# A two-block transformer kernel: expert rows added into X by TensorE inside the expert loop, and the cross attention's value projection moved behind the experts

## The chip, the cores and the metric

One core of one Trainium2 chip runs the whole program. The metric is device time in microseconds, the median of the runs shown. A core has TensorE (matrix products, PE in the rows), VectorE (DVE), ScalarE (ACT), GpSimd (POOL) and SyncE (SP), which only issues transfers. All of them run their own instruction stream and meet at semaphores.

## The reference

Two blocks follow one another on x of 512 tokens by 1024. Only the parts around the change are shown; everything is fp32.

```python
# first block: attention, then the experts
h2 = rms_norm(x, norm2_g[l]) * (1.0 + scale2) + shift2
# each token takes 2 of 32 experts (1024 -> 512 -> 1024); weights = g_prob * softmax(top 2 logits)
def expert_block(xb, e):
    return (jax.nn.silu(xb @ w_gate[e]) * (xb @ w_up[e])) @ w_down[e]
out = jnp.zeros((t, d)).at[row_token].add(ys * row_weight[:, None])
x = x + gate2[:, None, :] * out
x = rms_norm(x, final_norm_g)
# second block
h = rms_norm_2(x, norm_mix_g);  x = x + hybrid_mixer(h, ...)      # convolution and sparse attention
h = rms_norm_2(x, norm_x_g);    x = x + cross_attention(h, mem, xq_w, xkv_w, xo_w)
h = rms_norm_2(x, norm_ffn_g);  x = x + swiglu(h, ffn_in_w, ffn_out_w)
return rms_norm_2(x, final_norm_g_2)
# in cross_attention: mem is 256 x 1024 and does not depend on x
k, v = jnp.split(mem @ wkv, 2, axis=-1)
```

## The kernel before

**Experts.** The 32 experts run as 16 pairs: expert p on array columns 0 to 63 and expert p + 16 on columns 64 to 127, with at most 64 tokens each (CAP). What does not fit would go through an overflow loop, which these inputs do not enter. For pair p, GpSimd gathers 128 rows of h2 from DRAM by `idx[:, p]` (L2559). TensorE runs `moe_up` (gate into bank 0, up into bank 1, L1037), then the transposes of the next pair's rows (`moe_transpose_x`, L1019), the transposes of a (`moe_transpose_a`, L1046) and `moe_down` (banks 4 and 5, L1058). ACT applies SiLU and copies the transposed rows (L1593, L1586); VectorE multiplies (`moe_multiply`, L2215), copies the transposed a (`moe_keep_a`, L2207) and multiplies the result with gate2 into Y (`moe_keep_y`, L2223). ACT's queue stores Y to `expert_rows` in DRAM (`moe_store`, L1597). Weights have one buffer per kind: slots 0 and 1 gate, 2 and 3 up, 4 and 5 down. SP issues the next gate, up and down pieces (L538) as soon as the semaphores `gate_full`, `up_full` and `down_full` tell that the old ones are used. All expert products are fp32.

**Adding the rows to X.** After pair 14 is stored, GpSimd gathers the rows of the pairs 0 to 14 for each token (eight indirect transfers, L2567), and VectorE adds each with its weight into X (`expert_rows`, L2241). Rows of the last pair are not stored; TensorE multiplies them by a weighted selection matrix (`weighted_rows`, L1086, fp32) and VectorE adds the banks (L2248). Since the gather may also name overflow rows, a stretch of zeros was stored into `expert_rows` early in the attention (L521). The weighted selection is formed by VectorE after the routing (`selection`, L2176 to L2181) and transposed by TensorE (L1007, kept at L2199).

**Between the blocks.** ACT squares X with sums (`norm`, L1408), VectorE scales X with the final gain (L2311), ACT squares again, VectorE writes the scaled XN4 (L1862), TensorE transposes it (L775), ACT and VectorE split it into high and low parts (L1444, L1884), and the first projection of the second block (glu_g0) starts.

**Projections of the second block.** Each fp32 product is three fp32r products of split operands (`split_product`, L720 to L722). A weight chunk of 2 MiB (1024 x 512) lies in one of two slots in turn. It is handled in two halves: ACT rounds a half to its high part (`split_weights`, L1436, two buffers), GpSimd subtracts to form the low part (`low_weights`, L2513), and TensorE uses both. A table (`HALVES`) names for every half what must be done before its high buffer is taken again: `half_used` for first halves, `proj_done` of the chunk for second halves. SP loads chunk c when the chunk before it in the same slot is used (`chunk`, L488). The order on ACT, GpSimd, SP and TensorE is written out by hand.

**Cross attention.** Its order was: transposes of mem (L775) with their split (L1761, L2452), key projection (`xk`, L1767), norm of X, value projection (`xv`, two chunks of two token tiles, L1773), transposes of the normed X, query projection (`xq`).

## Time and profile before

| | |
|---|---|
| median of 3 runs | 2162.72 us (2159.34 to 2164.78) |
| profiled execution, its own time | 2158.53 us |
| its span, first to last instruction | 2156.7 us |
| mean granted TensorE clock | 0.946 of 2.4 GHz |
| busy: TensorE, VectorE, ACT, GpSimd | 88%, 31%, 27%, 29% of the span |
| bytes moved by DMA | 379.24 MB, mean 176 GB/s |

The execution can be cut by time: attention of the first block until about 385 us, routing until 432, experts until 922, norms until 955, then the second block; its cross attention begins at 1573. A busy share says little by itself: each stage has its own limit, and what counts there is which wait ends last. The rows further down show start and duration in microseconds, and in square brackets how long the engine sat idle before and who ended that.

### The profile page before, as it was taken

The numbers are of one execution on the slowest core, as the hardware profiler recorded it, in microseconds if no ns is written. First come the engines' busy times: TensorE is split into PE (matmuls) and PEld (weight loads), VectorE is DVE, ScalarE is ACT, GpSimd is POOL, SyncE is SP. The second block draws the span as 40 slices with busy tenths as digits, with TensorE's granted clock in tenths as the row PEclk, the third lists the DMA queues.
The fourth block names the chain that finished last, engine by engine and source line by source line (L and its number), as shares of the span: only waits on it lengthen the run. The fifth ranks groups of instructions, "written<-read, shape, count | busy, mean of one in ns | idle before, by whom it ended". The sixth has DMA issues, their size and how long they took to land.

```text
span 2156.7 us, 21339 instructions
## 1 busy us (share of the span) xinstructions
PE 1900.6 (88%) x8492; PEld 1229.5 (57%) x8492; DVE 671.8 (31%) x1383; ACT 582.9 (27%) x1042; POOL 629.6 (29%) x361
## 2 busy tenths in 40 slices
PE   4999989488778778769999999888889889999997
PEld 2544337333222222248888878544677578888886
DVE  6551265610011001155897024465211211000001
ACT  3113462110000000042231243566243423222211
POOL 0001233300000000124442224555364324555532
PEclk8999899699999999989997998999999999999999
DMA  9453301889999999932222312000233122232221
GB/s 376 156 229 110 124 1 64 331 338 424 428 428 427 430 428 428 424 131 93 103 86 71 120 57 98 20 21 21 98 122 113 40 88 78 78 112 84 94 102 59
DMA packets 94291, 379.24 MB, mean 176 GB/s; under 512 B 6219, under 2 KB 35275, under 8 KB 79868
## 3 DMA queue, kind: packets, MB, share of 16 engines
q1 hardware_dynamic: 88176, 356.99, 42.5%
q0 software_dynamic: 3456, 12.58, 1.5%
q10 hardware_dynamic: 2572, 8.46, 1.0%
q8 instruction: 60, 0.98, 0.2%
q14 instruction: 27, 0.22, 0.0%
HBM read 357.50 MB, written 20.51 MB: 175 GB/s over the span
## 4 chain that ended last, share of the span: by engine, by line
PE 70%; DMA 16%; DVE 7%; ACT 4%; issue 2%; POOL 1%; SPq 0%; DVEq 0%; ACTq 0%; POOLq 0%
PE bank L720 14%; PE bank L722 14%; PE bank L721 14%; DMA slots<-in_w_expert_up 14%; PE bank L695 11%; PE bank L1037 6%; PE bank L1252 2%; PE bank L1232 1%; PE bank L848 1%; ACT area L1749 1%; POOL low_r L2513 1%; DMA slots<-in_w_ada 1%; PE bank L766 1%; PE bank L1221 1%; PE bank L775 1%
## 5 line engine op out<-in xcount | busy, mean ns | idle before, releaser
L2513 POOL TENSOR_TENSOR low_r<-slots,high_r 128x2048 fp32r<-128x2048 f32 x87 | 401.1, 4611 | 605.7 <-ACT high_r L1436 605.7
L721 PE MATMUL bank<-xl_r,high_r 128*128 128x512 f32 (+1 forms) x864 | 330.6, 383 | 0.0
L720 PE MATMUL bank<-area_r,high_r 128*128 128x512 f32 x800 | 314.2, 393 | 0.0
L1037 PE MATMUL bank<-slots,area 128*64 128x512 f32 x992 | 247.0, 656 | 75.6 <-DMA slots<-in_w_expert_gate 39.0
L722 PE MATMUL bank<-area_r,low_r 128*128 128x512 f32 x800 | 312.5, 391 | 0.0
L1436 ACT ACTIVATE high_r<-slots 128x2048 fp32r<-128x2048 f32 x87 | 166.2, 1913 | 434.7 <-PE bank L722 413.8
L1037 PEld LDWEIGHTS bank<-slots,area 128*64 128x64 f32 x992 | 76.8, 151 | 245.2 <-issue 151.1
L721 PEld LDWEIGHTS bank<-xl_r,high_r 128*128 128x128 f32 x864 | 163.4, 189 | 31.9 <-issue 0.5
L720 PEld LDWEIGHTS bank<-area_r,high_r 128*128 128x128 f32 x800 | 151.1, 189 | 31.9 <-issue 0.5
L722 PEld LDWEIGHTS bank<-area_r,low_r 128*128 128x128 f32 x800 | 150.9, 189 | 31.6
L2339 DVE SCALAR_TENSOR_TENSOR bank<-area,cols,bank 128x512 f32<-128x512 f32 x232 | 153.4, 747 | 0.0
L695 PE MATMUL bank<-slots,area 128*128 128x512 f32 (+2 forms) x384 | 132.7, 499 | 2.0 <-ACT slots L1523 1.3
L1058 PE MATMUL bank<-slots,area 128*64 128x512 f32 x512 | 115.1, 602 | 19.3 <-DMA slots<-in_w_expert_down 8.7
L2559 POOL DMA_INDIRECT area<-h_rows,idx x16 | 15.6, 973 | 396.8 <-PE bank L1019 381.1
L722 PE MATMUL bank<-high_r,area_r 128*128 128x512 f32 x304 | 120.8, 397 | 0.0
L2215 DVE TENSOR_TENSOR area<-bank,area 128x512 f32<-128x512 f32 x16 | 11.1, 692 | 322.6 <-PE bank L1037 322.6
L695 PEld LDWEIGHTS bank<-slots,area 128*128 128x128 f32 x384 | 67.4, 193 | 60.0 <-issue 56.0
L695 PE MATMUL bank<-area 64*128 64x512 f32 (+3 forms) x150 | 72.1, 676 | 19.5 <-ACT area L1454 13.0
L1593 ACT ACTIVATE area<-bank 128x512 f32<-128x512 f32 x16 | 9.6, 597 | 291.4 <-PE bank L1037 291.4
L1058 PEld LDWEIGHTS bank<-slots,area 128*64 128x64 f32 x512 | 37.6, 138 | 85.7 <-issue 81.9
L2603 POOL TENSOR_SCALAR area<-area,small 128x128 f32<-128x128 f32 (+3 forms) x112 | 64.4, 585 | 69.4 <-DVE small L2418 69.4
L2484 DVE TENSOR_TENSOR area<-bank,area 128x512 f32<-128x512 f32 x22 | 15.2, 692 | 222.9 <-PE bank L722 222.9
(389 smaller groups left out, 2711.9 us busy)
## 6 DMA issues: line engine op xcount, KB each, us to landing
slots<-in_w_expert_up SPq DMA_DIRECT2D x32, 2048.0 KB, 19.6
slots<-in_w_expert_down SPq DMA_DIRECT2D x32, 2048.0 KB, 19.7
slots<-in_w_expert_gate SPq DMA_DIRECT2D x30, 2048.0 KB, 18.3
slots<-in_w_in SPq DMA_DIRECT2D x15, 2048.0 KB, 8.5
slots<-in_w_ada SPq DMA_DIRECT2D x11, 2048.0 KB, 12.5
slots<-in_ffn_in_w SPq DMA_DIRECT2D x22, 1024.0 KB, 7.1
slots<-in_ffn_out_w SPq DMA_DIRECT2D x5, 2048.0 KB, 7.8
slots<-in_w_out SPq DMA_DIRECT2D x4, 2048.0 KB, 7.9
```

The lines of the kernel that those rows point to most:

```text
L695: last = nc.tensor.matmul(out, lhsT, rhs, start=(n == 0), stop=(n == len(pairs) - 1))
L720: nc.tensor.matmul(out, xh, yh, start=start and n == 0, stop=False)
L721: nc.tensor.matmul(out, xh, yl, start=False, stop=False)
L722: last = nc.tensor.matmul(out, xl, yh, start=False, stop=stop and n == len(pairs) - 1)
L766: last = nc.tensor.transpose(banks[6 + n % 2][0:rows, c0:c0 + P], src, ID)
L1037: last = nc.tensor.matmul(banks[which][piece, :], XT[b][:, k, piece], w[side][:, k, :], start=k == 0, stop=k == KT - 1)
L1058: last = nc.tensor.matmul(banks[4 + half][piece, :], AT[b][:, k, piece], w[side][:, k, half * C:(half + 1) * C], start=k == 0, stop=k == 3)
L1252: last = nc.tensor.matmul(bank[64 * a:64 * a + 64, j * P:C], VV[:, j, c0:c0 + 64], PTN[hb % 2][a][:, j, j * P:C], start=False, stop=(branc ...
L1436: nc.scalar.activation(high_half(m), raw_half(m), ACT.Copy).then_inc(s["w_high"], 1)
L2339: ins = nc.vector.scalar_tensor_tensor(acc if j < CONV_W - 1 else CV[:, u, :], V[:, u, j:j + S], tap, acc, ALU.mult, ALU.add)
L2513: nc.gpsimd.tensor_tensor(low_half(m), raw_half(m), high_half(m), ALU.subtract).then_inc(s["w_low"], 1)
L2603: nc.gpsimd.tensor_scalar(NSA_P[a][i], NSA_P[a][i], rcp[:, at:at + 1], GS[:, i, gate:gate + 1], ALU.mult, ALU.mult).then_inc(s["nsa_probs" ...
```

## The change

The expert rows no longer go through DRAM. `moe_keep_y` now multiplies with the weight of each slot (`slot_weight`) and gate2 in one operation into a single Y; ACT rounds it to `Y_HIGH`, GpSimd forms `Y_LOW`, both fp32r. VectorE builds for each pair a 0/1 selection of 128 slots by 512 tokens by comparing token numbers (`moe_select`). TensorE multiplies selection and Y in two fp32r matmuls per piece of 128 tokens by 512 columns, eight pieces per pair, in banks 3 and 2 in turn; pieces of pair p − 1 are put between the gate and up matmuls of pair p, one after every second k. VectorE adds each piece to X. The store, the eight row gathers, the zero store and its memset are gone. VectorE's loop is unrolled. `moe_transpose_a` uses bank 2 and so waits for all eight adds.

The value projection `xv` moves from the cross attention to behind the experts: mem is loaded into slot 3 and the `xv` weights into slots 0 and 1 as the last pair frees them; mem is transposed and split there (a second time later, for the keys); its eight row groups come in order before the transposes of `mix`, and its result is stored to DRAM (`xv_dram`) and loaded again in the cross attention. The gate chunk glu_g0 now waits for the first `xv` chunk's slot.

```diff
@@ plan and HALVES: xv in front of glu_g0
+plan("xv", ["act"] * 4, 2)
 for _n in range(2):
     plan(f"glu_g{_n}", ["act"] * 4, 1)
...
-plan("xv", ["act"] * 4, 2)
@@ SyncE
-            sp.wait_ge(s["zeros_set"], 1)
-            sp.dma_start(ys_dram[(N_PAIR - 1) * P:, :].rearrange("(b p) d -> p b d", p=P),
-                         bass.AP(slots, 3 * SLOT, [[N_SLOTS * SLOT, P], [0, N_OVER + 1], [1, D]])
-                         ).then_inc(s["zeros_stored"], 16)
...
+            sp.wait_ge(s["up_full"], N_PAIR)
+            sp.dma_start(MTOK_EARLY, io["mem_2"][0].rearrange("(t p) d -> p t d", p=P)).then_inc(s["mem_loaded"], 16)
+            sp.wait_ge(s["gate_full"], N_PAIR)
+            halves("xv", xkv, 1024)
             sp.wait_ge(s["down_full"], 2 * N_PAIR)
...
             for n in range(2):
                 chunk(CHUNK_NO[f"glu_g{n}"], ...)
                 chunk(CHUNK_NO[f"glu_a{n}"], ...)
+                if n == 0:
+                    sp.wait_ge(s["act_emptied"], emptied("act", FIRST["xv"] + 3))
+                    sp.dma_start(xv_dram, XV_EARLY.rearrange("p a b -> p (a b)")).then_inc(s["xv_stored"], 16)
...
             halves("xk", xkv, 0)
-            halves("xv", xkv, 1024)
+            sp.wait_ge(s["xv_stored"], 16)
+            sp.wait_ge(s["tile_high"], 3 * KT)
+            sp.dma_start(XV.rearrange("p a b -> p (a b)"), xv_dram).then_inc(s["xv_loaded"], 16)
             halves("xq", xq, 0)
@@ TensorE
+            def expert_rows(out, n, b):
+                half, t = n // TT, n % TT
+                piece = slice(half * C, (half + 1) * C)
+                chosen = SELECT[b][:, t * P:(t + 1) * P]
+                nc.tensor.matmul(out, chosen, Y_HIGH[:, piece], start=True, stop=False)
+                return nc.tensor.matmul(out, chosen, Y_LOW[:, piece], start=False, stop=True)
+
+            def rows_before(p, n, b):
+                half, t = n // TT, n % TT
+                if n == 0:
+                    pe.wait_ge(s["selected"], p)
+                if t == 0:
+                    pe.wait_ge(s["y_low"], 2 * p - 1 + half)
+                at_least(pe, s["rows_added"], 8 * p - 9 + n)
+                expert_rows(banks[ROW_BANKS[n % 2]][:, :], n, 1 - b).then_inc(s["rows_full"], 1)
@@ moe_up, after both sides of k
-                    last.then_inc(s[full_sem], 1)
+                        if k == KT - 1:
+                            last.then_inc(s[full_sem], 1)
+                        if k % 2 and not (isinstance(p, int) and p == 0):
+                            rows_before(p, TT * which + k // 2, b)
@@ after the last pair
+            pe.wait_ge(s["mem_loaded"], 16)
+            for c in range(KT):
+                if c < 2:
+                    pe.wait_ge(s["y_ready"], 2 * N_PAIR - 1 + c)
+                split_transposes(XP["mem_early"] + c, ...)
+            pe.wait_ge(s["selected"], N_PAIR)
             for n in range(2 * TT):
+                if n == TT:
+                    split_emptied("mem_early")
                 if n % TT == 0:
+                    pe.wait_ge(s["y_low"], 2 * N_PAIR - 1 + n // TT)
+                expert_rows(banks[n][:, :], n, 1).then_inc(s["weighted_full"], 1)
+            pe.wait_ge(s["rows_added"], 8 * N_PAIR - 4)
+            for n in range(2):
+                split_token_major("xv", MTS_EARLY, C, n, tiles=2)
             split_norm_transposes("mix", XN4)
@@ ScalarE
-            def moe_store(p, b):
-                act.wait_ge(s["y_ready"], 2 * p + 2)
-                act.dma_start(rows[:, bass.ds(p, 1), :], Y[:, b:b + 1, :]).then_inc(s[f"y_stored{b}"], 16)
+            def moe_high_y(p):
+                at_least(act, s["rows_full"], 8 * p)
+                for half in range(2):
+                    act.wait_ge(s["y_ready"], 2 * p + 1 + half)
+                    nc.scalar.activation(Y_HIGH[:, piece], Y[:, piece], ACT.Copy).then_inc(s["y_high"], 1)
...
+            split_weights(FIRST_HALF["xv"] + 1)
...
             nc.scalar.activation(small[:, 153:154], small[:, 152:153], ACT.Sqrt)
+            for c in range(KT):
+                nc.scalar.activation(MTS_EARLY[0][:, c, :], split_transposed(XP["mem_early"] + c)[:, 0:MEM], ACT.Copy)
+            split_weights(FIRST_HALF["xv"] + 2)
             norm(XN3, s["x_moe"], 1)
+            split_weights(FIRST_HALF["xv"] + 3)
             norm(XN4, s["x_final"], 1)
-            split_weights(FIRST_HALF["glu_g0"] + 1)
+            split_weights(FIRST_HALF["xv"] + 4)
+            for n in range(4):
+                if n == 2:
+                    split_weights(FIRST_HALF["glu_g0"] + 1)
+                empty(nc.scalar.activation(XV_EARLY[:, n % 2, n // 2 * C:n // 2 * C + C], full(FIRST["xv"] + n)[:, :], ACT.Copy))
@@ ScalarE, cross attention: norm(XN4) now ahead of the copies of xk; the copies of xv are gone
@@ VectorE
+            for p in range(N_PAIR):
+                if p:
+                    for n in range(2 * TT):
+                        dve.wait_ge(s["rows_full"], 8 * p - 7 + n)
+                        add_rows(n, banks[(3, 2)[n % 2]]).then_inc(s["rows_added"], 1)
+                moe_multiply(p, p % 2)
+                moe_keep_a(p, p % 2)
+                moe_select(p, p % 2)
+                moe_keep_y(p)
@@ GpSimd
+            for p in range(N_PAIR):
+                if p + 3 < N_PAIR:
+                    gather_rows(p + 3)
+                for half in range(2):
+                    pool.wait_ge(s["y_high"], 2 * p + 1 + half)
+                    nc.gpsimd.tensor_tensor(Y_LOW[:, piece], Y[:, piece], Y_HIGH[:, piece], ALU.subtract)
```

After the routing, `selection` (three operations on 1024 and 512 columns) is replaced by `HI_WEIGHT` (two on 248), four additions on 128 columns (`IOTA4`) and small copies; the four transposes of the selection by eight small accumulating products (`LO` by `HI_WEIGHT`, 31 columns).

## Rows read from the trace of the kernel before

**Rows 1.** The page, strip of 40 slices of 53.9 us: what DMA moved.

```profile
GB/s 376 156 229 110 124 1 64 331 338 424 428 428 427 430 428 428 424 131 93 103 86 71 120 57 98 20 21 21 98 122 113 40 88 78 78 112 84 94 102 59
```

**Rows 2.** Busy time by window, the pair with a gather and the one without.

```profile
core 0: us, PE busy (x) PEld busy (x) DVE busy (x) ACT busy (x) POOL busy (x), PEclk, DMA share, GB/s
617.90:649.70 31.80, 25.47 (x108) 8.74 (x108) 2.76 (x4) 1.68 (x3) 0.94 (x1) 0.89 1.01 428
840.70:871.30 30.60, 22.86 (x108) 8.62 (x108) 2.77 (x4) 1.68 (x3) 0.00 (x0) 1.00 1.01 429
```

**Rows 3.** Waits of TensorE in one pair: us in total, times, longest.

```profile
PE bank L1037 <- DMA slots<-in_w_expert_gate: 3.8, 1, 3.8
PE bank L1037 <- DMA slots<-in_w_expert_up: 1.4, 1, 1.4
```

**Rows 4.** The chain that ended last, one piece: start, duration, what.

```profile
625.43 24.23 DMA slots<-in_w_expert_up
```

**Rows 5.** Timeline from the last down products to the first gate projection.

```profile
913.15 8.78 PE L1058 MATMUL bank<-slots,area 128*64 128x512 f32 x32 [2.62 <-issue]
...
930.18 1.06 ACT L1408 ACTIVATE area<-X 128x1024 f32<-128x1024 f32 x1 [29.63 <-DVE X L2248]
...
941.88 6.98 DVE L1862 TENSOR_SCALAR area<-X,small 128x1024 f32<-128x1024 f32 x4
...
943.51 4.79 POOL L2513 TENSOR_TENSOR low_r<-slots,high_r 128x2048 fp32r<-128x2048 f32 x1 [2.65 <-ACT high_r L1436]
...
948.91 6.41 PE L775 MATMUL bank<-k,area 128*128 128x128 f32 x32 [19.91 <-DVE area L1862]
...
955.07 0.48 PE L720 MATMUL bank<-area_r,high_r 128*128 128x512 f32 x1
```

**Rows 6.** Busy time by window, 50 us of the gate projections.

```profile
1000.00:1050.00 50.00, 50.00 (x223) 41.38 (x222) 43.10 (x66) 10.79 (x9) 23.08 (x5) 1.00 0.36 126
```

**Rows 7.** Timeline of the cross attention, mem tiles to transposes.

```profile
1573.88 1.21 ACT L1761 ACTIVATE lent_r<-bank 128x256 fp32r<-128x256 f32 x4 [9.19 <-PE bank L775]
...
1601.88 0.28 PE L722 MATMUL bank<-lent_r,low_r 128*128 128x256 f32 x1
...
1610.30 2.74 DVE L1862 TENSOR_SCALAR area<-X,small 128x1024 f32<-128x1024 f32 x4
...
1628.56 1.91 PE L775 MATMUL bank<-k,area 128*128 128x128 f32 x16
```

**Rows 8.** Transfers of the whole span: KB each, median us to landing.

```profile
expert_rows<-area ACTq DMA_DIRECT2D x15, 512.0 KB, 10.2
...
slots<-in_xq_w SPq DMA_DIRECT2D x2, 2048.0 KB, 7.8
```

**Rows 9.** Timeline of one pair, from up to the next gate.

```profile
617.88 7.09 PE L1037 MATMUL bank<-slots,area 128*64 128x512 f32 x32 [2.50 <-DMA slots<-in_w_expert_up]
...
625.17 0.69 DVE L2215 TENSOR_TENSOR area<-bank,area 128x512 f32<-128x512 f32 x1 [21.33 <-PE bank L1037]
...
627.83 7.09 PE L1058 MATMUL bank<-slots,area 128*64 128x512 f32 x32 [1.17 <-DMA slots<-in_w_expert_down]
...
638.74 9.62 PE L1037 MATMUL bank<-slots,area 128*64 128x512 f32 x32 [3.82 <-DMA slots<-in_w_expert_gate]
```

**Rows 10.** Timeline of TensorE in the router: half-array products between transposes.

```profile
393.07 1.08 PE L970 MATMUL bank<-area 128*64 128x512 f32 x4
...
394.08 1.09 PE L766 MATMUL bank<-k,area 128*128 128x128 f32 x8
```

**Rows 11.** Timeline from the control words to the first expert transposes.

```profile
417.09 3.62 PE L695 MATMUL bank<-area 128*128 128x31 f32 x16 [4.46 <-DVE area L2157]
...
424.86 1.23 DVE L2176 TENSOR_TENSOR area<-late,small 128x1024 f32<-128x1024 f32 x1
...
430.07 1.94 PE L1019 MATMUL bank<-k,area 128*128 128x128 f32 x8 [0.83 <-DVE area L2199]
```

**Rows 12.** The page: ACT's rounding of half a weight chunk (count, busy, mean ns).

```profile
L1436 ACT ACTIVATE high_r<-slots 128x2048 fp32r<-128x2048 f32 x87 | 166.2, 1913 | 434.7 <-PE bank L722 413.8
```

More of the change, by code:

```diff
@@ L346, in build @@
         GATE1 = [A(8192, SLOT), A(8192 + SLOT, SLOT)]
[L347 to L350 removed]
+        Y, Y_LOW, Y_HIGH = A(16624, D), AR(16624, D), AR(17648, D)
+        HI_WEIGHT = A(19704, 8 * N_BLOCKS, 8)
+        IOTA4 = A(20992, C)
+        SELECT = [AR(18672, C), AR(19184, C)]
+        OV_EQ, OV_SEL, OV_WSEL, OV_Y = A(12528, 1024), A(13552, C), A(14064, C), A(14576, D)
+        OV_W = [slot(4), slot(5), GATE1[0]]
+        MTOK_EARLY = slots[:, 3 * SLOT:3 * SLOT + 2048].rearrange("p (a b) -> p a b", a=2)
+        MTS_EARLY = (AR(12528, 2048, KT), AR(14576, 2048, KT))
+        XV_EARLY = E(0, 2048, 2)
         last_dest = small[:, 244:252]
@@ L579, in _, with halves @@
                 up_and_down_weights(p)
+            w2, pw, wo2 = w3(io["w_in_2"][0]), w3(io["conv_pw_w_2"][0]), w3(io["w_out_2"][0])
+            xq, xkv, xo = w3(io["xq_w_2"][0]), w3(io["xkv_w_2"][0]), w3(io["xo_w_2"][0])
+            ffin, ffout = w3(io["ffn_in_w_2"][0]), w3(io["ffn_out_w_2"][0])
+            def halves(stage, w, first):
+                for n in range(2):
+                    chunk(CHUNK_NO[stage] + n, [(0, w[:, :, first + n * C:first + (n + 1) * C])])
+            sp.wait_ge(s["up_full"], N_PAIR)
+            sp.dma_start(MTOK_EARLY, io["mem_2"][0].rearrange("(t p) d -> p t d", p=P)).then_inc(s["mem_loaded"], 16)
+            sp.wait_ge(s["gate_full"], N_PAIR)
+            halves("xv", xkv, 1024)
             sp.wait_ge(s["down_full"], 2 * N_PAIR)
@@ L594, in _ @@
             sp.dma_start(E(6144, 2048), io["cmp_w1_flat"][:, 0, :]).then_inc(s["extras_loaded"], 16)
-            w2, pw, wo2 = w3(io["w_in_2"][0]), w3(io["conv_pw_w_2"][0]), w3(io["w_out_2"][0])
-            xq, xkv, xo = w3(io["xq_w_2"][0]), w3(io["xkv_w_2"][0]), w3(io["xo_w_2"][0])
-            ffin, ffout = w3(io["ffn_in_w_2"][0]), w3(io["ffn_out_w_2"][0])
-            def halves(stage, w, first):
-                for n in range(2):
-                    chunk(CHUNK_NO[stage] + n, [(0, w[:, :, first + n * C:first + (n + 1) * C])])
             for n in range(2):
@@ L1005, in _ @@
             bank = bank_of(FIRST["select"])
-            for t in range(TT):
-                last = nc.tensor.transpose(bank[:, t * P:(t + 1) * P], SELECT[:, t * P:(t + 1) * P], ID)
-            last.then_inc(s["proj_done"], 1)
+            accumulate(bank[:, 0:N_BLOCKS], [(LO[:, n, :], HI_WEIGHT[:, n, :]) for n in range(8)]
+                       ).then_inc(s["proj_done"], 1)
             all_emptied(FIRST["select"] + 1)
@@ L1288, in _ @@
                 split_feature_major("xk", MTS, n, tokens=MEM)
-            for n in range(2):
-                split_token_major("xv", MTS, C, n, tiles=2)
             split_norm_transposes("normx", XN4)
@@ L1769, in _ @@
                     split_weights(FIRST_HALF["xk"] + c // 4 * 2 + 4)
-            norm(XN4, s["dve_emptied"], emptied("dve", FIRST["wo2"] + 4))
-            for n in range(4):
-                split_weights(FIRST_HALF["xv"] + n // 2 * 2 + 3)
-                empty(nc.scalar.activation(XV[:, n % 2, n // 2 * C:n // 2 * C + C], full(FIRST["xv"] + n)[:, :], ACT.Copy))
-                if n == 1:
-                    split_weights(FIRST_HALF["xv"] + 4)
             split_weights(FIRST_HALF["xq"] + 2)
@@ L2196, in _ @@
             then(nc.vector.tensor_copy(ctl[:, N_OVER:N_OVER + 1], RS(1216 + 31, 1)))
-            selection(last_dest, EQ, SELECT).then_inc(s["onehot_ready"], 1)
+            dve.wait_ge(s["pool_step"], 2)
+            for t in range(TT):
+                nc.vector.tensor_scalar(IOTA4[:, t * P:(t + 1) * P], IOTA, float(t * P), None, ALU.add)
             bank = full(FIRST["select"])
-            nc.vector.tensor_copy(WSEL, bank[:, :]).then_inc(s["dve_emptied"], 1)
+            nc.vector.tensor_copy(slot_weight[:, :], bank[:, 0:N_BLOCKS]).then_inc(s["dve_emptied"], 1)
+            dve.wait_ge(s["dve_emptied"], emptied("dve", FIRST["slots"]))
+            then(nc.vector.tensor_copy(slot_token[:, :], idx[:, :]))
             nc.vector.memset(small[:, 154:155], 0.0).then_inc(s["ctl_ready"], 1)
@@ L2237, in expert_rows @@
-            def expert_rows(t):
-                dve.wait_ge(s[f"yg_loaded{t}"], 32)
-                for a in range(2):
-                    then(nc.vector.scalar_tensor_tensor(X[:, t, :], YG[2 * t + a], wts[:, a, t:t + 1], X[:, t, :],
-                                                        ALU.mult, ALU.add))
-            def add_weighted(n):
+                    nc.vector.scalar_tensor_tensor(Y[:, piece], banks[4 + half][:, :], slot_weight[:, p:p + 1],
+                                                   gate2[:, piece], ALU.mult, ALU.mult).then_inc(s["y_ready"], 1)
@@ L2257, in _, with add_weighted @@
-            for half in range(2):
-                dve.wait_ge(s["down_full"], 2 * p + 1 + half)
-                piece = slice(half * C, (half + 1) * C)
-                nc.vector.tensor_tensor(Y[:, 1, piece], banks[4 + half][:, :], gate2[:, piece], ALU.mult
-                                        ).then_inc(s["y_ready"], 1)
-                expert_rows(2 + half)
+                return nc.vector.tensor_tensor(X[:, t, piece], X[:, t, piece], bank[:, :], ALU.add)
+            def add_weighted(n):
+                return add_rows(n, banks[n])
@@ L2555, in _, with gather_rows @@
             pool.wait_ge(s["h2_stored"], 64)
-            for p in range(N_PAIR):
+            def gather_rows(p):
                 if p >= 2:
```

139 lines of the change are left out of this document (63 added, 76 removed), and 4 rows, old and new, of the table at.

## The prediction

> **What bounds the kernel now.** I read the strip of 40 slices first. From slice 10 to 17 the transfers run at 424 to 430 GB/s and nowhere else for long [rows 1]; those are the expert pairs. One pair there lasts 31.80 us at 428 GB/s with a DMA share of 1.01. The last one of the loop has no gather and lasts 30.60 us at the same rate [rows 2]. The bytes agree: six weight pieces of 2 MiB are 12.58 MB, the gather and the store of the expert rows 0.524 MB each; 13.63 MB at 428 GB/s are 31.8 us, and one half-megabyte less is 1.22 us, which is the difference seen. In the pair, TensorE waits for the gate weights 3.8 us and the up weights 1.4 us [rows 3], and an up piece issued at 625 lands after 24.2 us, most of it queue [rows 4]. So DMA sets the pair, with some 14 us of queue as reserve, and TensorE has about 6 us to spare. Behind the last pair come the gathered rows, the adds and two norms, TensorE idle for 19.9 us [rows 5]. From there on TensorE is full (50.00 of 50 us) [rows 6]. In the late cross attention it alternates with the splitting of weights, and the value projection stands between the keys and the norm's transposes [rows 7].
>
> **The pair loop.** Removed: 15 stores of 512 KiB [rows 8], each 1.22 us of a full queue. Their place is taken by nothing on DMA. The new period on DMA is 30.6 us. On TensorE, gate, up and down take 7.09 us each at full clock, and from the end of up to the start of down 2.86 us pass (624.97 to 627.83) [rows 9]: 24.1 us. (The gate in these rows took 9.62, partly at the lower clock level behind 3.8 us of idleness; with fuller work the granted clock was 1.00 [rows 2].) Added: 16 fp32r matmuls of 512 columns. In the dense stretch 223 of these take 50 us, 0.224 each: 3.6 us [rows 6]. They come as eight pairs of matmuls between fp32 matmuls on array halves. Going back and forth between array halves and the full array is shown once: a burst of two half-array products takes 1.01 us start to start (393.07 to 394.08) where half-array products alone run 0.43 each [rows 10, 9], so 0.15 for a switch and back; eight are 1.2 us. Last, VectorE has to add the eighth piece before it multiplies: 0.7 us more, less what TensorE does meanwhile, 0.7 net. Sum 29.6 us, 1.0 under the DMA's 30.6. The eight adds (0.69 each, as L2215 in [rows 9]), the row selection and two products are some 9 us of VectorE in 30. On GpSimd two subtractions of a quarter of 4.8 us [rows 5] stand behind the gather three ahead, which waits only for transposes already passed. ACT's copies of Y stand behind the x copies, before the next SiLU; they are ready 3 us before the gate. All hidden. If the switch costs nothing the period is still 30.6; if it costs 0.5, TensorE needs 32.4 and sets it. I take 0.15, the only row near it.
>
> Here the Trainium skill ("TensorE: Matmul & The Clock Gate", Part 3, on the mechanism of row and column tiling) speaks against the change: a weight load overlaps running matmuls only if the row groups differ. All loads here use all rows. In the dense stretch the loads last 0.186 us each and the matmuls still come every 0.224 [rows 6], so the trace does not follow that rule for full-array work; by the page's load figure (about 107 ns for 128 columns, an estimate of 1.7 us per pair) the period would be 31.3. The rival below is worked out from rows.
>
> **The start.** Two one-hot operations of 1.23 us, a sum of 0.69, four transposes, and a copy of 0.69 stood between the control words and the first expert transposes (424.86 to 430.07) [rows 11]. In their place stand four small additions, small copies, and 16 small matmuls, as those that form the slots (3.62 us) [rows 11], which run beside VectorE. That is 4 us if the first gathered rows are there, 2 if not; I take 3. The zero store and its memset lie in the attention, where no weights stand behind them (the slice after it moves 1 GB/s [rows 1]): nothing.
>
> **The last pair.** Before, down ends at 913.15 + 8.78 = 921.93 [rows 5], 50.6 us behind the start of the last loop pair's up (871.3) [rows 2]. New: 29.6 to the next up, 7.09 and three interruptions (1.8), then 4.1 to down, 7.09: 49.7. With 14 stores before that (17.1) and the start (3.0) down ends 21.0 earlier, at about 901.
>
> **From the last down to the first gate projection.** Before: 955.07 − 921.93 = 33.1 us [rows 5]. The eight row gathers vanish from the chain, but the value projection stands in front. Count from down's end. VectorE, ACT and GpSimd form Y and its parts until 3. ACT splits the first half weight (1.9 [rows 12]), loads the square-root table (now not hidden), and copies eight memory tiles of 0.35 (four in 1.21 with their overlap, and a semaphore each [rows 7]): 8.2; TensorE's rows and VectorE's adds end at 13 to 16. The first norm's squares start 3 us later than before (8.2 in [rows 5]). The four halves of the projection are 24 matmuls each, 5.5 us. The third half's split waits for the first half to be used (17 to 22) and stands on ACT ahead of the second norm's squares; GpSimd then needs 4.6 for its low part, so TensorE does the third at 24 to 33. The fourth half's split stands behind the second norm: low part ready at 31 to 35, products until 36 to 40. Only then come the transposes (6.2 [rows 5]): 42.5 to 46.5. I take 44.5, so 11.4 us are given back. The gate weights load after the second half (23 to 27), 8 us [rows 8], split and low by 38 to 41: just hidden. Of the 22 us of products some 15 lie under the norms, but ACT and GpSimd make them too late to fit fully.
>
> Inside this stretch, VectorE's four scalings took 6.98 us where a GpSimd subtraction began meanwhile [rows 5], and 2.74 where none did [rows 7]. The Trainium skill ("SBUF — State Buffer", on the shared port pair) calls it an exclusive lock for a whole instruction; the trace agrees. By it one scaling of the first norm could stand behind the third half's low part, 4 us more, the upper end of the range above with 4 added.
>
> **The late projection.** The key products end at 1602.0, transposes begin at 1628.56 [rows 7]. All between is the value projection: 22 us of products and 4.6 of waits for low weights and loads. Without it the transposes follow at once, if the norm is there: its squares now stand ahead of the key copies and delay the third key half's split by 0.9 us at most. The query weights load one chunk earlier, in time. The saved values (1 MiB) are loaded behind the keys' second chunk, with 100 us to go. Gain 26.0.
>
> **Sum.** −21.0 + 11.4 − 26.0 = −35.6 us, from 2158.5 (the profiled execution, span 2156.7): 2122.9. The median shown is 4.2 higher, so I give 2127. Differences under 0.3%, 6.5 us, can't be told from none here.
>
> **Rivals.**
> 1. TensorE becomes the bound of the pairs (0.19). The two resources stand only 1.0 us apart. Each 0.1 us on an interruption is 0.8 per pair; at 0.35 each the period is 31.2, at 0.43 it is 31.8 and the loop gives nothing: −17, 2146. For it: eight switches per pair and sixteen waits in one stream. Against: the 0.15 measured.
> 2. Slower than before (0.07): the same place, but an interruption drains the array, because matmuls on halves, full array and semaphore waits don't mix. Outside the loop 19 us are gained (3.0 + 0.9 + 26.0 − 11.4); it decides from a period of 33.5, 0.64 us per interruption; at 34.5 the time is 2180. Against it: router bursts mixed at 0.15 [rows 10].
> 3. The projection behind the experts fits nowhere (0.05, inside the main case's upper range): splits and lock push the gate stage to 55 after down: −25, 2138.
> 4. Full-array weight loads do not hide beside half-array products (0.04): 0.186 us exposed sixteen times in a pair is 3.0, the period 32.6, the loop loses 12 us instead of gaining 18, −5 in all, 2157: no measurable change. For it: no row here loads the full array during half-array products. Against: hidden in [rows 6]. It is the weight-load rule of the Trainium skill page named above.
> 5. The change gives nothing because 1 and 3 come together (0.03).
> 6. The start and the tail both go at their best: −41 and more (0.04).
>
> The main case (TensorE just under DMA) has 0.58 and spans 2117 to 2135. Range for 8 in 10: 2113 to 2147, from the best start and tail to the loop without gain. Faster 0.86, same 0.07, slower 0.07.
>
> **What the new profile must show.** Pair period 30.6 at 428 GB/s, and TensorE still waiting for gate or up weights, under 1.5 us together. Up and gate phases of 9.2 to 9.5 us at clock 1.0. If the GB/s of the slices falls under 420, rival 1 holds. First expert transposes at 427; last down at 901; TensorE idle in three pieces in the 44 us after it, one of them before the fourth half; gate projection at 945; transposes directly behind the keys in the late part. I am wrong if the pair is above 31.2 us or the first gate product is more than 50 us behind the last down.

## The result

The changed kernel takes 2134.57 us (median of 4 runs, 2132.41 to 2138.23), the one before 2162.36 beside it on the same chip (2159.34 to 2164.78): a ratio of 0.9877 [0.9864, 0.9891], 27.8 us less. Forecast were 2127 and 35.6 us less. The profiled execution after took 2138.23 us (span 2136.3), the slowest of its four; its span is only 20.4 us under that of before, and the positions below come from it. Run again later the same kernel took 2135.46 (2134.66 to 2136.05), 25.6 under before, with a span of 2133.6. Where its two traces differ, both are given. The first trace's span gives less than the medians because the profiled execution of before lies 3.8 us under its median and the one after 3.7 above.

The page's strip (what DMA moved, slices of 53.4 us), against [rows 1]:

```profile
GB/s 380 158 231 79 0 1 64 322 286 426 427 427 427 430 428 427 379 166 84 88 110 79 99 79 50 60 29 23 60 138 79 40 89 79 79 119 79 103 94 60
...
HBM read 355.41 MB, written 5.31 MB: 169 GB/s over the span
```

The rate of the transfers in the pairs is the same; seven slices are full of it instead of eight. Two windows of the pairs, against [rows 2]:

```profile
490.00:520.00 30.00, 28.73 (x126) 10.16 (x124) 8.60 (x14) 2.94 (x5) 3.41 (x4) 1.00 1.00 427
860.00:890.00 30.00, 28.73 (x126) 10.17 (x124) 8.60 (x14) 2.94 (x5) 2.54 (x2) 1.00 1.01 428
```

And what TensorE waits for from 440 to 912 (total, times, longest), against [rows 3]:

```profile
PE bank L1091 <- DVE area L2259: 12.5, 16, 0.8
PE bank L1079 <- DVE area L2267: 8.2, 15, 1.4
...
PE bank L1066 <- DMA slots<-in_w_expert_gate: 0.4, 1, 0.4
```

TensorE is busy 28.7 of 30 us and waits for a weight once, 0.4 us. (L1066 is gate and up, L1038 and L1039 are the two products of a row piece, L1079 the transposes of a, L1091 down; on VectorE L2287 is the adds, L2267 the multiplication, L2259 the copy of the transposed a.) Yet the transfers run at a share of 1.00. When a pair's up weights are issued shows the period:

```profile
447.73 0.80 SPq L538 DMA_DIRECT2D slots<-in_w_expert_up  x2
476.64 0.80 SPq L538 DMA_DIRECT2D slots<-in_w_expert_up  x2
...
566.92 0.81 SPq L538 DMA_DIRECT2D slots<-in_w_expert_up  x2
597.02 0.81 SPq L538 DMA_DIRECT2D slots<-in_w_expert_up  x2
...
868.79 0.81 SPq L538 DMA_DIRECT2D slots<-in_w_expert_up  x2
```

After the first pair it is 30.1 us, but for two steps near the end of 30.46 and 30.67; the 14 steps take 421.1. Before, the same steps were 25.8, 24.1, 31.3, 31.9 and so on, 448.14 to 880.14: 432.0. An up piece lands after 13.3 us (median) at 500 to 560 and after 18.3 at 760 to 820: the transfers fall behind by half a microsecond a pair. They need 30.6 and are asked for 30.1; the reserve of loaded weights pays, and in the step of 30.67 it is used up.

The way from the last down product to the gate stage, against [rows 5] (L1479 rounds a half of the weights, L1671 loads ACT's table, L1673 copies the memory's tiles, L785 is transposes, L1451 the norm's squares, L2355 the scalings of X, L2555 the low part of a half of the weights, L730 the first of three products, at 944.36 of the value projection and at 956.16 of the gate projection):

```profile
902.42 7.09 PE L1091 MATMUL bank<-slots,area 128*64 128x512 f32 x32 [0.78 <-DVE area L2259]
...
910.88 1.89 ACT L1479 ACTIVATE high_r<-slots 128x2048 fp32r<-128x2048 f32 x1
...
912.79 1.28 ACT L1671 ACT_TABLE_LOAD   x1
...
914.19 1.19 ACT L1673 ACTIVATE area_r<-bank 128x256 fp32r<-128x256 f32 x4
...
915.07 1.97 PE L785 MATMUL bank<-k,slots 128*128 128x128 f32 x8 [3.83 <-DVE area_r L2339]
...
921.81 1.06 ACT L1451 ACTIVATE area<-X 128x1024 f32<-128x1024 f32 x1 [2.55 <-DVE X L2287]
...
926.77 9.21 DVE L2355 SCALAR_TENSOR_TENSOR X<-X,small,area 128x1024 f32<-128x1024 f32 x4
...
929.89 5.00 POOL L2555 TENSOR_TENSOR low_r<-slots,high_r 128x2048 fp32r<-128x2048 f32 x1 [5.93 <-ACT high_r L1479]
...
944.36 0.79 PE L730 MATMUL bank<-high_r,area_r 128*128 128x512 f32 x1 [3.62 <-POOL low_r L2555]
...
956.16 0.47 PE L730 MATMUL bank<-area_r,high_r 128*128 128x512 f32 x1
```

Down ends at 909.51, the gate stage begins 46.65 us later (46.79 in the second trace), not 33.1. The row products are held behind the memory's transposes, these behind ACT's copies, these behind a weight split and a table load; so the first norm square is 12.3 us behind down instead of 8.2. The first row products also come at the lower clock, behind 3.8 us in which TensorE stood: from 916.70 to 920.30 the granted clock is 0.50, the level of 1.2 GHz.

Position by position, in us against before (after; second trace of it):

| | forecast | first trace | second trace |
|---|---|---|---|
| first expert transposes | −3.0 | −1.0 | −3.8 |
| from there to the end of the last down | −18.0 | −11.4 | −11.6 |
| last down to first gate projection | +11.4 | +13.5 | +13.7 |
| gate projection to the memory's transposes (618.4 before) | 0 | +4.6 | +4.7 |
| memory's transposes to first query projection (62.05 before) | −26.0 | −26.3 | −26.3 |
| the rest | 0 | +0.2 | +0.2 |
| sum | −35.6 | −20.4 | −23.1 |

### The profile page after: what moved, and what is told of

Same layout as the page of the kernel before. It is cut to its first block, busy times and chain, and to the rows that moved or that the text cites. A ratio compares the mean times of both kernels' runs of the same rounds, so it can differ in the third digit from the quotient of the medians.

```text
span 2136.3 us, 22123 instructions
## 1 busy us (share of the span) xinstructions
PE 1971.8 (92%) x8760; PEld 1255.7 (59%) x8760; DVE 760.2 (36%) x1522; ACT 604.5 (28%) x1082; POOL 662.3 (31%) x384
## 4 chain that ended last, share of the span: by engine, by line
PE 81%; DVE 7%; ACT 5%; DMA 4%; issue 2%; POOL 1%; DVEq 0%; SPq 0%; ACTq 0%
PE bank L730 14%; PE bank L731 14%; PE bank L732 14%; PE bank L705 11%; PE bank L1066 10%; PE bank L1091 5%; PE bank L1038 2%; DMA slots<-in_w_expert_gate 2%; PE bank L1296 2%; PE bank L1276 2%; PE bank L858 1%; PE bank L1039 1%; ACT area L1808 1%; POOL low_r L2555 1%; DMA slots<-in_w_ada 1%
## 5 line engine op out<-in xcount | busy, mean ns | idle before, releaser
L2555 POOL TENSOR_TENSOR low_r<-slots,high_r 128x2048 fp32r<-128x2048 f32 x87 | 400.9, 4608 | 609.8 <-ACT high_r L1479 609.8
L730 PE MATMUL bank<-area_r,high_r 128*128 128x512 f32 x800 | 313.9, 392 | 0.7 <-POOL low_r L2555 0.7
L1479 ACT ACTIVATE high_r<-slots 128x2048 fp32r<-128x2048 f32 x87 | 166.2, 1912 | 427.5 <-PE bank L732 419.0
L1066 PE MATMUL bank<-slots,area 128*64 128x512 f32 x992 | 240.1, 607 | 1.2 <-ACT area L1627 0.7
L730 PEld LDWEIGHTS bank<-area_r,high_r 128*128 128x128 f32 x800 | 151.0, 189 | 32.6 <-POOL low_r L2555 1.0
L2287 DVE TENSOR_TENSOR X<-X,bank 128x512 f32<-128x512 f32 x128 | 87.6, 687 | 219.2 <-PE bank L1039 219.2
L1066 PEld LDWEIGHTS bank<-slots,area 128*64 128x64 f32 x992 | 62.2, 137 | 123.9 <-issue 119.1
L732 PE MATMUL bank<-high_r,area_r 128*128 128x512 f32 x336 | 133.0, 396 | 0.0
L1091 PE MATMUL bank<-slots,area 128*64 128x512 f32 x512 | 113.4, 595 | 12.5 <-DVE area L2259 12.5
L2614 POOL TENSOR_TENSOR area_r<-area,area_r 128x512 fp32r<-128x512 f32 x32 | 40.7, 1273 | 188.6 <-ACT area_r L1641 188.6
L705 PE MATMUL bank<-area 64*128 64x512 f32 (+3 forms) x166 | 77.4, 661 | 19.3 <-ACT area L1497 12.8
L2528 DVE TENSOR_TENSOR area<-bank,area 128x512 f32<-128x512 f32 x22 | 15.2, 692 | 222.9 <-PE bank L732 222.9
L1091 PEld LDWEIGHTS bank<-slots,area 128*64 128x64 f32 x512 | 35.3, 137 | 79.5 <-issue 64.0
```

The source lines that it names most:

```text
L705: last = nc.tensor.matmul(out, lhsT, rhs, start=(n == 0), stop=(n == len(pairs) - 1))
L730: nc.tensor.matmul(out, xh, yh, start=start and n == 0, stop=False)
L732: last = nc.tensor.matmul(out, xl, yh, start=False, stop=stop and n == len(pairs) - 1)
L1066: last = nc.tensor.matmul(banks[which][piece, :], XT[b][:, k, piece], w[side][:, k, :], start=k == 0, stop=k == KT - 1)
L1091: last = nc.tensor.matmul(banks[4 + half][piece, :], AT[b][:, k, piece], w[side][:, k, half * C:(half + 1) * C], start=k == 0, stop=k == 3)
L1479: nc.scalar.activation(high_half(m), raw_half(m), ACT.Copy).then_inc(s["w_high"], 1)
```

## The experiments

Four kernels first, to part the two halves of the change and to find what bounds the pair.

**The rows alone.** All edits of `xv` are undone: it is planned, loaded and multiplied where it stood before.

```diff
-            halves("xv", xkv, 1024)
...
             halves("xk", xkv, 0)
+            halves("xv", xkv, 1024)
```

> The change of the expert rows alone; the value projection of the cross attention stands where it stood before. Theory (the projection behind the experts is mostly paid for there): the loop is as in the changed kernel (last down product ends near 909.5), from there to the first gate projection 34 to 36 us instead of 46.65, and the late stretch from the memory's transposes to the first query projection is 62 us again; time = 2134.6 + 26.3 - 11.6 = about 2149. Rival (the rows themselves, with their high and low parts, make the long end of the experts): 44 us or more to the first gate projection, time near 2134.6 + 26 - 2 = 2159.

2147.3 us (2144.69 to 2148.09), ratio 0.9930 [0.9916, 0.9943]. The loop is that of the changed kernel: first to last up issue 420.9 us. From the last down (907.95) to the gate projection (937.26) it takes 29.3 us, less than the 34 to 36 expected and less than the 33.1 of before: the new rows are also a shorter tail than eight gathers. From the memory's transposes to the query projection it takes 63.85. So the early projection costs 17.3 us behind the experts and brings 28.1 in the cross attention, 10.8 net; the medians differ by 12.7. The rival, that the rows make the long tail, falls. In this trace the norm runs free:

```profile
912.33 1.06 ACT L1432 ACTIVATE area<-X 128x1024 f32<-128x1024 f32 x1 [1.10 <-DVE X L2259]
...
917.28 4.87 DVE L2321 SCALAR_TENSOR_TENSOR X<-X,small,area 128x1024 f32<-128x1024 f32 x4
...
931.06 6.44 PE L775 MATMUL bank<-k,area 128*128 128x128 f32 x32 [18.10 <-DVE area L1888]
```

(L1432 is the squares, L2321 the scalings, L775 the transposes.) The first square is 4.4 us behind down, the scalings take 4.87 us and not 9.21, and TensorE idles for 18.1 us: the room in which the projection was to fit.

**Four interruptions.**

```diff
-                        if k % 2 and not (isinstance(p, int) and p == 0):
-                            rows_before(p, TT * which + k // 2, b)
+                        if not (isinstance(p, int) and p == 0):
+                            for n in ({3: (0, 1), 7: (2, 3)}, {3: (4, 5), 6: (6, 7)})[which].get(k, ()):
+                                rows_before(p, n, b)
```

> The eight row pieces of a pair are put in at four places (two pieces each, after the fourth and eighth k of gate, the fourth and seventh of up) instead of eight. Theory 1 (each change between the half-array float32 products and the full-array float32r products costs about 0.36 us, however many float32r products stand together, and TensorE sets the pair at 30.1): a pair costs TensorE 30.1 - 4 x 0.36 = 28.7; the DMA engines, which need 30.6 a pair and have been busy all the time, then become the bound once their reserve is used, so the last down product comes 8 to 12 us earlier and not 15 x 1.44 = 21: time about 2123 to 2128, and waits for up or gate weights in the last third of the loop. Theory 2 (the price belongs to each piece, its semaphore wait or its two matmuls): pair stays at 30.1, time 2133 to 2136.

2133.55 us (2133.04 to 2134.78), ratio 0.9869 [0.9854, 0.9884]. That is in the range of theory 2 and above the 2123 to 2128 of theory 1, but the trace speaks for theory 1. The up issues:

```profile
476.31 0.80 SPq L538 DMA_DIRECT2D slots<-in_w_expert_up  x2
...
562.61 0.81 SPq L538 DMA_DIRECT2D slots<-in_w_expert_up  x2
593.26 0.81 SPq L538 DMA_DIRECT2D slots<-in_w_expert_up  x2
...
867.84 0.81 SPq L538 DMA_DIRECT2D slots<-in_w_expert_up  x2
```

And its TensorE's waits:

```profile
PE bank L1066 <- DMA slots<-in_w_expert_gate: 15.6, 12, 1.6
...
PE bank L1066 <- DMA slots<-in_w_expert_up: 5.5, 12, 0.8
```

The pair drops to 28.3 us (476.31, 504.62, 532.94) and from the fifth on is 30.64, with the waits for weights back. So the price sits on the interruption, as theory 1 said, and DMA takes over from the fifth step on; but the whole is worth 1.2 us over the 14 steps (419.9), not 8 to 12: here theory 1 was wrong. The changed kernel had only a microsecond left to gain there. One interruption in each kernel, first the changed one:

```profile
609.95 1.94 PE L1066 MATMUL bank<-slots,area 128*64 128x512 f32 x8
611.82 0.50 PE L1038 MATMUL bank<-area_r 128*128 128x512 f32 x1
612.15 0.40 PE L1039 MATMUL bank<-area_r 128*128 128x512 f32 x1
612.48 1.94 PE L1066 MATMUL bank<-slots,area 128*64 128x512 f32 x8
```

```profile
489.11 0.50 PE L1038 MATMUL bank<-area_r 128*128 128x512 f32 x1
489.45 0.39 PE L1039 MATMUL bank<-area_r 128*128 128x512 f32 x1
489.68 0.39 PE L1038 MATMUL bank<-area_r 128*128 128x512 f32 x1
489.91 0.40 PE L1039 MATMUL bank<-area_r 128*128 128x512 f32 x1
490.24 3.65 PE L1066 MATMUL bank<-slots,area 128*64 128x512 f32 x16
```

Half-array products come 0.43 us apart by twos, so eight take 1.72. From one group to the next it is 2.53: 0.15 more ahead of the first fp32r product, 0.33 and 0.33 for the two where 0.23 is their rate. That is 0.36 an interruption. Four products in one cost 0.33, 0.23, 0.23, 0.33, again with 0.15 ahead of the first: the same 0.36.

**No low parts.** `expert_rows` makes one product with `Y_HIGH`; the one with `Y_LOW` is left out.

> The product with the low parts of the rows is left out, so each piece is one float32r matmul instead of two (the sum in X lacks the low part). Theory 1 (price per interruption): the cadence of eight half-array products and one piece goes from 2.53 to 2.30, a pair to 28.3 by TensorE, later 30.6 by DMA; time 2121 to 2127. Theory 2 (price per float32r matmul): the extra 0.36 halves too, the cadence goes to 2.12.

(The products are L1038 alone, and gate and up are L1065 here.) 2131.8 us (2130.19 to 2132.86), ratio 0.9863 [0.9848, 0.9878].

```profile
490.55 1.94 PE L1065 MATMUL bank<-slots,area 128*64 128x512 f32 x8
492.42 0.50 PE L1038 MATMUL bank<-area_r 128*128 128x512 f32 x1
492.85 1.94 PE L1065 MATMUL bank<-slots,area 128*64 128x512 f32 x8
```

The cadence is 2.30, as theory 1 had it. The pair is 28.2, then 30.6, and the time is above the 2121 to 2127 expected: again DMA keeps what TensorE gives (the 14 steps take 418.3).

**With stores.** 512 KiB a pair are written to a scratch tensor again.

```diff
                 moe_high_y(p)
+                act.dma_start(ys_dram.rearrange("(b p) d -> p b d", p=P)[:, bass.ds(p, 1), :],
+                              gate2.rearrange("p (a d) -> p a d", a=1)).then_inc(s["y_stored"], 16)
```

> The changed kernel with a store of 512 KiB per pair added back (a constant tile to a scratch tensor; nothing waits for it but the end of the loop). Theory 1 (TensorE sets the pair at 30.1, while the DMA engines need 30.6 and live on a reserve that shrinks 0.5 us a pair): DMA need is 31.8 a pair again, the reserve of about 10 us is used up in 6 or 7 pairs and then the pair is 31.8, so the loop ends 8 to 14 us later: time 2143 to 2149. Theory 2 (DMA has slack at 30.1): less than 3 us. Theory 3 (the DMA engines set 30.1 already): 14 x 1.2 = 17 to 24 us, time 2152 or more.

2149.66 us (2145.38 to 2151.34), ratio 0.9947 [0.9931, 0.9963]. The pair is 30.1 at first and 31.8 from the sixth step on; the 14 steps take 436.05 (444.51 to 880.56), 15.0 more. That lies just above the 8 to 14 of theory 1 and well above "less than 3". The bytes count nearly in full (14 × 1.22 = 17.1), although a window shows TensorE as the bound: the reserve was already spoken for.

Three kernels on the stretch behind the experts.

**Late low parts.**

```diff
-            low_weights(FIRST_HALF["xv"] + 4)
+            low_weights(FIRST_HALF["xv"] + 2)
             pool.wait_ge(s["x_final"], 4)
+            low_weights(FIRST_HALF["xv"] + 4)
```

> The changed kernel, but GpSimd forms the low parts of the third and fourth half of the value weights only when VectorE has scaled all four rows of X. Theory 1 (the scaling of X, which reads two operands from SBUF, and GpSimd's low part shut each other out: 9.21 us for four scalings beside it, 4.87 in the kernel with the rows alone): the four scalings take 4.9 us, the second norm ends 4.3 us earlier, the third low part starts at 931.7 instead of 929.9; the first gate projection comes 2 to 4 us earlier and the time is 2131 to 2133. Theory 2 (the long scalings have another cause, the traffic of the transfers or of ScalarE): still 9 us, and TensorE gets its third half 1.8 us later: time 2135 to 2137.

2132.15 us (2128.92 to 2134.76), ratio 0.9869 [0.9851, 0.9886]; 44.27 us from down to gate.

```profile
924.42 4.87 DVE L2355 SCALAR_TENSOR_TENSOR X<-X,small,area 128x1024 f32<-128x1024 f32 x4
...
929.37 4.54 POOL L2555 TENSOR_TENSOR low_r<-slots,high_r 128x2048 fp32r<-128x2048 f32 x1 [7.90 <-DVE X L2355]
```

With GpSimd held back the four scalings take 4.87 us. So 4.3 of the 9.21 were VectorE standing behind one GpSimd instruction, and 2.4 of them reach the end of the stretch, inside the 2 to 4 expected. The time itself moved by less than the runs scatter; the trace decides here.

**Order 1** and **order 2**, in words (one line for each queue, before and after; 1 and 2 mark where they differ):

```
-            halves("xv") behind the load of mem_2      +  ahead of it
-            PE: 8 memory transposes, rows 0..7 in 8 banks
+            PE: 4 memory transposes, rows 0..7 in banks n % TT, 4 memory transposes
-            ACT: moe_high_y; split xv 0; Sqrt; 8 copies; split xv 1; squares; split xv 2; norm XN4
+            ACT: split xv 0; Sqrt; moe_high_y; 4 copies; split xv 1; squares; 4 copies; norm XN4; split xv 2   (1)
+            ACT: the same, but 4 copies ahead of the squares, split xv 2 ahead of norm XN4                    (2)
-            DVE: 8 low parts, 8 adds
+            DVE: 8 adds, 4 low parts, scalings, 4 low parts   (1)      4 low parts, 8 adds, 4 low parts   (2)
```

> The changed kernel with the stretch behind the experts in another order: the value weights are issued ahead of the memory, ScalarE splits their first half and loads its table ahead of the last pair's high parts, TensorE transposes four of the memory's eight tiles, then makes the last row pieces in four banks, then the other four tiles; VectorE adds the rows ahead of the memory's low parts. Theory 1 (of the 17.3 us that the value projection costs there against the kernel with the rows alone, 7.9 lie ahead of the first norm square, because the row pieces stand behind all eight transposes, their copies, a weight split and a table load): the first square starts about 5 us behind the last down product instead of 12.3, the second norm ends near 936 and the first gate projection comes 39 to 42 us behind the last down product instead of 46.65: time 2128 to 2131. Theory 2 (GpSimd's four low parts of 4.6 us and TensorE's 22 us set the end of the stretch, whatever the order of the norms): less than 2 us, time 2133 to 2135.

> As tail1, but VectorE forms the memory's first four low parts ahead of the adds, ScalarE copies the other four tiles ahead of the norm's squares, and the third half is split ahead of the second norm, so that TensorE starts the value projection about 2 us earlier and the norms end about 4 us later. Theory 1 (the norms set the end): slower than tail1 by 2 to 4 us. Theory 2 (TensorE and GpSimd with the value projection set the end): faster than tail1 by 1 to 3 us.

Order 1: 2134.08 us (2126.96 to 2135.3), ratio 0.9867 [0.9847, 0.9886]. The first square starts 6.3 us behind down (913.71) and XN4 is complete at 933.65, counted from down 9.1 us earlier than in the changed kernel, but the gate projection only 2.3 us (44.31). The value products had lost what the norm won: they begin 18.8 us behind down instead of 12.7, because TensorE waits 3.4 us for the memory's last low parts, which VectorE forms behind the scalings, and the first 14 of them come at the lower clock (0.50 from 926.20 to 932.20) behind that wait. Their third low part began at 928.25, behind the second norm on ACT. Order 2: 2129.61 (2128.66 to 2134.11), ratio 0.9858 [0.9838, 0.9878], but 45.97 from down to gate: the scalings were back at 9.21. Both also loaded an ACT table three times (1.28 each), with the dummy square root ahead of a branch; behind the branch, where order 3 has it again, there is one load. Order 1 missed its 39 to 42 us, and for order 2 trace and median point opposite ways (1.7 us later, 4.5 less), so neither theory wins outright. My reading is that the chain ACT, GpSimd, TensorE of the four halves sets the end, and that the norm matters through the order on ACT and through the lock; order 3 tests it. The medians can't rank them.

**Order 3** joins what each trace had shown: order 2, the table load where it was, the low parts held as above. Beside it the changed kernel again, and order 3 with four interruptions.

> The changed kernel once more, beside the two others of this call on one chip, to see what a difference of 2 or 3 us is worth and what its profiled execution does in the stretch from the first gate projection to the memory's transposes, which was 4.6 us longer than before in the first one. If that was an accident of the granted clock in one execution, the stretch is 618 to 620 us here; if it belongs to the change, 623 again. Time 2133 to 2136.

> The order of tail2, with the table load behind the last pair's high parts, where it was, and GpSimd's third and fourth low parts held until X is scaled, as in late_low. Theory 1 (the end of the stretch is set by the four value products on TensorE, each behind its high part on ScalarE and its low part on GpSimd, and the port decides when the third may start): scalings of X 4.9 us, no product waits more than 3 us for its low part, first gate projection 39 to 42 us behind the last down product instead of 46.65; time 4.5 to 7.5 us under the changed kernel of the same call. Theory 2 (the transfers for the gate weights, which are issued only when the first value chunk is used up, set the end): 44 us or more and a gate projection that waits for its weights or their low part; less than 3 us.

> tail3 with the row pieces put in at four places a pair, as in four_groups. The two edits lie in different stretches and the loop gains 1 us by it (the DMA engines set 30.64 a pair there), so the time is 0 to 2 us under tail3.

On one chip: the changed kernel 2135.46 us (ratio 0.9882 [0.9867, 0.9897]), order 3 2126.69 (2125.55 to 2129.53; 0.9841 [0.9827, 0.9854]), with four interruptions 2127.85 (2126.5 to 2131.24; 0.9849 [0.9836, 0.9863]).

```profile
910.16 9.16 POOL L2568 TENSOR_TENSOR low_r<-slots,high_r 128x2048 fp32r<-128x2048 f32 x2
...
921.85 4.87 DVE L2368 SCALAR_TENSOR_TENSOR X<-X,small,area 128x1024 f32<-128x1024 f32 x4
...
926.80 4.55 POOL L2568 TENSOR_TENSOR low_r<-slots,high_r 128x2048 fp32r<-128x2048 f32 x1 [7.48 <-DVE X L2368]
933.51 4.88 POOL L2568 TENSOR_TENSOR low_r<-slots,high_r 128x2048 fp32r<-128x2048 f32 x1 [2.16 <-ACT high_r L1484]
...
948.73 0.47 PE L730 MATMUL bank<-area_r,high_r 128*128 128x512 f32 x1
```

The first two low parts come without a gap, the scalings run free, and TensorE waits for a low part once, 2.9 us. Down to gate is 41.35 us instead of 46.79: 5.4. The span is 6.0 shorter, the median 8.8 (4.5 to 7.5 were expected), so some 3 us of the median are scatter. Theory 1 of that run holds; the four interruptions add nothing that can be told. Every run of order 3 lies under every run of the changed kernel beside it, by 5 us or more, and by 28 under those of before.

## Why the prediction came out as it did

The time lies in the range, on the forecast side, 7.6 us above the point. The main case, TensorE just under DMA, holds, though with 30.1 against 30.64 and not 29.6 against 30.6; neither sign of being wrong came (a pair above 31.2 us, the gate product more than 50 behind down). Several positions were missed all the same: down ends at 909.5 and 906.5 in the two traces instead of 901, the gate projection starts at 956.2 and 953.3 instead of 945. The reasons, by its steps:

- **The start, −3.0.** About right in size (−1.0 and −3.8), and it varies: the first expert transposes stand at 425.8 to 427.5 in nine of the eleven traces with the new rows, at 429.1 and 429.8 in two; before at 430.07. They now wait for the first gather (5.12 us in the first trace), which I had named as the condition.
- **"Removed: 15 stores, each 1.22 us of a full queue", −17.1.** This is the term that was mis-sized: the 14 steps gave 10.9. The bytes are right (with the stores back it costs 15.0). What failed is taking the pair as DMA-bound from the first. The first pairs run from loaded weights and are as fast as TensorE: 25.8 and 24.1 us before, 28.9 and 30.1 now. The slots come free later, and DMA, out of work, shows a share of 0.59 and 210 GB/s from 470 to 480 where it was 0.99 before: 4.1 us of transfers lost. Four interruptions give 1.2 back, 0.5 of it in this same gap (the share is then 0.64), so TensorE's own pace costs some 0.7 beside it; about 1.4 of the 6.2 are not traced.
- **The price of a switch, 0.15.** It is 0.36, so rival 1's picture (TensorE sets the pair) is what the windows show: 30.1 and not 29.6, with TensorE busy throughout. At its "0.35 each the period is 31.2" the sum was 1.1 too high: I had 7.09 each for gate, up and down where start to start they take 6.9 (0.6 together), and 3.56 from up to down with the last add where it is 3.07. The consequence of rival 1 did not come: 30.1 is still under DMA's 30.64, measured in two experiments, so the sum is set by DMA all the same. The sign I gave for it, GB/s under 420, could not have shown it either, since the reserve keeps DMA at its full rate. The row I took the price from, the router's burst, changes between two fp32 operations and counts start to start, so it holds the way to the full array alone. That part is 0.15 here too; the 0.2 at the ends of the first and the last fp32r product was left out.
- **The last pair, −0.9.** From the last issue of up weights to the end of down it was 41.8 us and is 40.7: −1.1.
- **The tail, +11.4.** 13.5: the gate projection comes 46.65 us behind down, inside the 42.5 to 46.5 only with the 4 us that were added for the lock. The order of events was as written; the rows' products start 7.2 us behind down and the norm at 12.3 instead of 11, and the lock that the prediction had put outside the sum is in it, 4.3 us, 2.4 of them to the end. The Trainium skill ("SBUF — State Buffer", on the shared port pair) says that a VectorE instruction with two inputs in SBUF and a GpSimd one that reads SBUF exclude each other for the whole instruction; the traces agree, 9.21 against 4.87 us. And 33.1 was not the right base for judging the move: the rows alone have 29.3, so the projection costs 17.3 there.
- **The late projection, −26.0.** 26.3.
- **No term at all** was there for the stretch from the gate projection to the memory's transposes. It is 623.0 and 623.1 us in the two traces of the changed kernel, 618.4 before. Windows of 25 us at equal distance from the first gate projection (325, 350, 550 and 575 us), before and then after:

```profile
1280.07:1305.07 25.00, 22.86 (x129) 19.64 (x127) 3.35 (x6) 18.98 (x28) 13.76 (x9) 0.95 0.29 106
1305.07:1330.07 25.00, 25.00 (x109) 22.15 (x109) 16.30 (x30) 4.45 (x5) 6.85 (x3) 0.78 0.00 0
1505.07:1530.07 25.00, 17.58 (x106) 9.88 (x107) 11.03 (x37) 10.25 (x32) 10.78 (x16) 0.96 0.15 53
1530.07:1555.07 25.00, 25.00 (x109) 20.61 (x108) 2.77 (x4) 3.83 (x2) 5.80 (x2) 0.97 0.27 94
```

```profile
1281.16:1306.16 25.00, 22.86 (x134) 19.45 (x133) 4.13 (x8) 19.38 (x30) 12.66 (x8) 1.00 0.29 106
1306.16:1331.16 25.00, 25.00 (x105) 21.93 (x105) 16.74 (x33) 5.16 (x6) 6.88 (x4) 0.73 0.00 1
1506.16:1531.16 25.00, 20.02 (x108) 9.78 (x106) 11.40 (x41) 10.63 (x33) 9.88 (x15) 0.86 0.00 1
1531.16:1556.16 25.00, 22.31 (x91) 18.29 (x92) 2.71 (x4) 2.55 (x2) 5.88 (x2) 0.93 0.34 126
```

  The last number but two of each row is the clock. In the first two windows what one lost the other gained, so they give nothing; in the last two 0.10 and 0.04 of 25 us are 3.5. The remaining 1.1 arise between 197 and 252 us behind the first gate projection, at a like clock: there TensorE waits 0.75 us for a low part (at 1215.23), which it does not before. But for the store of the early values (1 MiB) near its start, that stretch was not changed. Order 2 had the clock of before in the last two windows and 618.4 us, the kernel with stores had 1.00 at 325 and 350 and 616.6, order 3 621.7: it goes with where the kernel's parts fall in time, not with its work. What decides it was not tried and stays open.

Of the rivals, 2 (slower), 3 (a tail of 55 us), 5 and 6 fell by the time or the positions. Rival 4 priced sixteen exposed loads of 0.186 us, 3.0 a pair; eight interruptions of 0.36 are 2.9, so the pair alone can't tell them apart. The experiments can: with one product an interruption, and so half the loads, the price is still 0.36, and with four the two in the middle follow every 0.23 us, each with a full load. The Trainium skill's rule on loads and row groups ("TensorE: Matmul & The Clock Gate", Part 3) would show as a longer cadence there, and doesn't. Whether the 0.15 ahead of the first product is its own load, the one that meets half-array products, no run shows.

## What to carry to other kernels

In a stretch in which the transfers are at their full rate, fewer bytes come back in full only if the transfers never run out of work: count the loop from first issue to last landing, with the reserve that is loaded ahead, and not as pairs times a period. When a second resource comes within 2% of the first, a window shows either as the bound; put the bytes back, or take work from the other, and see which moves the end. Work that is moved under a stall costs more than its own operations: its splits and copies stand in the queues ahead of the chain that made the stall, so write the order of each queue anew before judging the place.

## What was not expected of the hardware

- Changing from float32 products on half the array to float32r products on the whole and back costs 0.36 us, whether one, two or four stand between (0.15 ahead of the first, about 0.1 at its end and at the last's).
- VectorE's four scalings of 1024 columns, with two operands from SBUF, take 4.87 us alone and 9.21 with one GpSimd subtraction of 2048 columns beginning among them.
- In unchanged code the granted clock of two neighbouring windows of 25 us moved from 0.96 and 0.97 to 0.86 and 0.93 when other parts of the kernel moved, the same in two runs of one kernel. The stretch of some 620 us around them took 616.6 us in the kernel with stores and 624.3 in the one with the rows alone.
